# Two more weight slots, a scale moved behind the token gather, and a first gather split by groups of four experts, in a two-layer encoder kernel

## The chip, the cores and the metric

The kernel runs on one core of a Trainium2 chip. The metric is the device time of one execution in microseconds. The kernel before took 790.39 us, the median of three runs (790.09 to 791.79).

## The reference

The input is 256 tokens of 1024 features in f32, behind which 16 learned meta tokens are put in front, so T = 272. There are two layers: layer 0 mixes tokens with a gated convolution and a gated linear attention, layer 1 with grouped-query attention. Each ends with a mixture of experts (MoE), in which each token goes to the best of 4 groups and in it to the best 2 of 8 experts. Cut to what the change touches:

```python
def rms_norm(x, g):
    y = x * lax.rsqrt(jnp.mean(x * x, axis=-1, keepdims=True) + NORM_EPS)
    return y * g

def hierarchical_moe(h, w_group, b_group, w_expert, b_expert, w_gate, w_up, w_down):
    g_logits = xt @ w_group + b_group                 # 4 groups, softmax, the largest is taken
    e_logits = (xt @ w_expert + b_expert)             # 8 experts in each group, the best two are taken
    gates = ...                                       # softmax of the two, times the group's probability
    for e in range(32):                               # F = 256
        he = jax.nn.silu(xt @ w_gate[e]) * (xt @ w_up[e])
        out = out + gates[:, e:e + 1] * (he @ w_down[e])

for i in range(2):
    h = h + mixer_i(rms_norm(h, norm_mix[i]))
    h = h + hierarchical_moe(rms_norm(h, norm_ffn[i]), ...)   # layer 1: without the meta tokens
return rms_norm(h, norm_final)
```

## The kernel before

**The weights.** The 32 experts of a layer have 96 MB of f32 weights, in 96 units of 1 MB (`UNITS`): three for each expert (gate, up, down). They pass through a ring of 16 slots in SBUF (`RING`, `slots`). Slots 0 to 7 are also the ring of the mixers' weights, and slots 8 to 15 lie over the mixers' scratch memory. So the first 16 units of a layer can be loaded only as the mixer ahead of it lets go of those places (`first_units0`, `first_units1`).

**The stages.** Experts are worked off in 8 quads of four. A quad has three stages of four units each (gate, up, down), 24 stages in all; in the first quad the two first stages hold each the halves (over the input features) of gate and up. TensorE raises `stage_done` at the end of each stage. SyncE, which issues all weight DMAs in one queue, waits for it before it overwrites a slot: unit i waits for the stage of unit i - 16 (`rest_of_units`, the DMA lines 356 and 359, and 353 for the halves of the first quad). In the first stage that frees slots, unit 16 is thus issued.

**The tokens.** A quad takes at most 32 tokens for each expert (`SLOTS`). The router yields `key`, each token's rank in its expert's queue. `select` (line 1085) makes from it `sel`, a matrix of ones and zeros of 256 columns (8 experts, that is two quads, times 32 places). `gather` (line 1701) multiplies the normalized tokens `hn` with `sel`: hn is TensorE's stationary operand, taken as `hn[:, t, c:D:8]`, so 128 elements that lie 8 elements apart in each partition, and `sel` the moving one. For two quads it needs 8 feature chunks c times NT token tiles t of such products: NT is 3 in layer 0 (one tile is the 16 meta tokens) and 2 in layer 1. Each f32 matmul stands in the trace as two records, each with its own weight load. `x_out` copies the result from PSUM to `xT`, with ScalarE from bank 0 and VectorE from bank 1 (line 1122). The stages' matmuls stand at line 1652 (gate, up) and 1688 (down), the transposes of `he` at 1677, those of the weighted selection at 1711, the scatter back at 1726, and its addition to h at 1131.

**The order on TensorE in the first pair of quads**, of a layer: route (1606, 1607), logits (1621), ranks (1628), loads of the experts (1632), `gather` of feature chunks 0 to 3, first stage, `gather` of chunks 4 to 7, second stage, transposes, down stage of quad 0. Quad 1 finds its tokens gathered. Each later pair is gathered in one piece of 8 chunks during the odd quad before it.

**The router.** VectorE works off a chain of small instructions (lines 1033 to 1070), each of which waits for the one before it. ScalarE takes the roots for the norm (508) and the second half of the logits out of PSUM (672). The product `before` / `ones` times `chosen` counts for each token those ahead of it in its expert's queue.

**The norm.** `hn` = h * 1/rms * gain is made by VectorE at line 836 for all norms (`scale_tile`), the first tiles of the MoE's norm among the additions that end the mixer. The gain lies in a tile of 4 KB in each partition, which GpSimd's queue loads anew before each norm.

## Time and profile before

| | us |
|---|---|
| median of the runs | 790.39 |
| profiled execution, its own time | 789.43 |
| its span | 787.6 |
| TensorE, matmul busy | 651.5 (83%) |
| VectorE busy | 251.3 (32%) |
| ScalarE busy | 156.6 (20%) |
| DMA | 234.95 MB, mean 298 GB/s |

The profiled execution took 1.8 us more than its span, and 1.0 us less than the median. "Matmul busy" is no measure of a limit, since matmuls are pipelined and each record holds its latency. The second part of the page cuts the span into 40 slices of 19.7 us; the row GB/s shows when the weights stream. The MoE of layer 0 streams from about 199 to 399 us, that of layer 1 from about 569 to 768 us. Times in the trace are microseconds from the start of the span.

### The profile page before, as it was taken

How to read it: one execution, taken by the hardware profiler on the slowest of the kernel's cores; microseconds unless marked ns; L12 is line 12 of the kernel's file. 1: busy time of each engine (PE TensorE's matmuls, PEld its weight loads, DVE VectorE, ACT ScalarE, POOL GpSimd, SP SyncE). 2: the span in 40 equal slices, each digit the busy share in tenths (PEclk: the TensorE clock that was granted, in tenths of full speed). 3: DMA queues.
4: the chain of work that ended last, by engine and by line, in shares of the span. 5: the costliest groups of instructions: out<-in, count | busy, mean ns of one | idle time of the engine just before them, and what ended most of it. 6: DMA issues, size and time to landing. Idle time of an engine off the chain costs nothing.

```text
span 787.6 us, 10827 instructions
## 1 busy us (share of the span) xinstructions
PE 651.5 (83%) x4656; PEld 389.1 (49%) x4656; DVE 251.3 (32%) x582; ACT 156.6 (20%) x328; POOL 42.9 (5%) x40
## 2 busy tenths in 40 slices
PE   2999998987999599599589989798888587677665
PEld 2796997346574274274224345544635235235221
DVE  4255335144224033023033557603322212212204
ACT  4563350030100000000003235712101001001002
POOL 3222251000000000000000000000000000000000
PEclk9999999997999899699799998999799979879888
DMA  9641345980899999999994360079299999999991
GB/s 305 244 149 67 107 125 177 391 321 28 361 421 422 421 421 420 422 421 419 420 395 157 109 195 19 1 264 377 74 423 421 421 421 422 421 422 419 422 412 76
DMA packets 46041, 234.95 MB, mean 298 GB/s; under 512 B 4465, under 2 KB 4721, under 8 KB 23457
## 3 DMA queue, kind: packets, MB, share of 16 engines
q1 hardware_dynamic: 44720, 231.82, 73.9%
q0 software_dynamic: 1264, 2.34, 1.2%
q8 instruction: 41, 0.67, 0.3%
q14 instruction: 16, 0.12, 0.0%
HBM read 233.07 MB, written 1.05 MB: 297 GB/s over the span
## 4 chain that ended last, share of the span: by engine, by line
PE 64%; DMA 21%; DVE 5%; SPq 4%; ACT 3%; issue 2%; DVEq 0%; ACTq 0%
DMA ring<-in_moe_w_up 20%; PE bank L1701 10%; PE bank L1652 10%; PE bank L1726 6%; PE bank L1688 5%; SPq L356 4%; PE bank L1351 4%; PE bank L1560 4%; PE bank L1785 4%; PE bank L1893 4%; PE bank L1352 3%; PE bank L1353 3%; PE bank L1792 2%; ACT scratch L779 2%; DMA gain<-in_norm_mix 1%
## 5 line engine op out<-in xcount | busy, mean ns | idle before, releaser
L1652 PE MATMUL bank<-ring,hnT 128*32 128x256 f32 (+1 forms) x1920 | 141.0, 454 | 75.9 <-DMA ring<-in_moe_w_up 41.2
L1652 PEld LDWEIGHTS bank<-ring,hnT 128*32 128x32 f32 x1920 | 70.3, 126 | 148.7 <-issue 61.1
L1701 PE MATMUL bank<-sel,hn 128*128 128x256 f32 x320 | 83.4, 421 | 0.3 <-DVE sel L1085 0.3
L1701 PEld LDWEIGHTS bank<-sel,hn 128*128 128x128 f32 x320 | 79.5, 337 | 3.8 <-issue 1.7
L1726 PE MATMUL bank<-moe_scratch 128*128 128x512 f32 (+1 forms) x160 | 78.1, 611 | 1.8 <-ACT moe_scratch L696 1.6
L1142 DVE TENSOR_TENSOR moe_scratch<-moe_scratch,bank 128x256 f32<-128x256 f32 x16 | 6.7, 422 | 198.8 <-ACT moe_scratch L690 198.8
L1131 DVE TENSOR_TENSOR h<-bank,h 128x512 f32<-128x512 f32 (+1 forms) x80 | 55.1, 689 | 23.7 <-PE bank L1726 23.7
L1688 PE MATMUL bank<-ring,moe_scratch 128*32 128x512 f32 x512 | 58.2, 595 | 1.5 <-DMA ring<-in_moe_w_down 1.1
L1351 PE MATMUL bank<-hnT_hi,mix_hi 128*128 128x272 f32 x160 | 47.7, 298 | 1.7 <-DVE scratch L972 1.7
L1726 PEld LDWEIGHTS bank<-moe_scratch 128*128 128x128 f32 (+1 forms) x160 | 22.7, 169 | 50.2 <-issue 26.3
L1352 PE MATMUL bank<-hnT_hi,mix_lo 128*128 128x272 f32 x160 | 46.8, 293 | 0.0
L1353 PE MATMUL bank<-hnT_lo,mix_hi 128*128 128x272 f32 x160 | 46.7, 292 | 0.0
L690 ACT ACTIVATE moe_scratch<-bank 128x256 f32<-128x256 f32 x16 | 6.1, 384 | 199.1 <-PE bank L1652 199.1
L1122 DVE COPY hnT<-bank 128x512 f32<-128x512 f32 x16 | 11.1, 692 | 77.9 <-PE bank L1701 77.9
L1351 PEld LDWEIGHTS bank<-hnT_hi,mix_hi 128*128 128x128 f32 x160 | 30.8, 192 | 3.5 <-DVE scratch L972 2.0
L1688 PEld LDWEIGHTS bank<-ring,moe_scratch 128*32 128x32 f32 x512 | 15.4, 109 | 31.6 <-issue 30.8
L1353 PEld LDWEIGHTS bank<-hnT_lo,mix_hi 128*128 128x128 f32 x160 | 30.8, 193 | 0.0
L1352 PEld LDWEIGHTS bank<-hnT_hi,mix_lo 128*128 128x128 f32 x160 | 30.8, 192 | 0.0
L1560 PE MATMUL bank<-ring,hnT 128*128 128x512 f32 x64 | 28.3, 597 | 0.3 <-ACT hnT L660 0.3
L295 POOL TENSOR_TENSOR mix_lo<-ring,mix_hi 128x2048 fp32r<-128x2048 f32 x5 | 24.0, 4803 | 79.5 <-ACT mix_hi L564 79.5
L1893 PE MATMUL bank<-ring,hnT 128*128 128x512 f32 x64 | 27.7, 594 | 0.5 <-ACT hnT L792 0.5
L1785 PE MATMUL bank<-ring,hnT 128*128 128x512 f32 x64 | 28.0, 595 | 0.0
(272 smaller groups left out, 696.1 us busy)
## 6 DMA issues: line engine op xcount, KB each, us to landing
ring<-in_moe_w_down SPq DMA_DIRECT2D x64, 1024.0 KB, 26.7
ring<-in_moe_w_gate SPq DMA_DIRECT2D x56, 1024.0 KB, 21.7
ring<-in_moe_w_up SPq DMA_DIRECT2D x56, 1024.0 KB, 25.9
ring<-in_sc_w_in SPq DMA_DIRECT2D x12, 1024.0 KB, 12.4
ring<-in_moe_w_gate SPq DMA_DIRECT2D x16, 512.0 KB, 6.7
ring<-in_moe_w_up SPq DMA_DIRECT2D x16, 512.0 KB, 7.9
ring<-in_att_w_in SPq DMA_DIRECT2D x6, 1024.0 KB, 20.5
ring<-in_sc_w_out SPq DMA_DIRECT2D x4, 1024.0 KB, 6.8
```

Source lines behind the costliest of these rows:

```text
L356: sp.dma_start(dst.rearrange("p (c n) -> p c n", c=KC), src).then_inc(sem(f"weights{l}_{stage_of(i) % 4}"), 16)
L1131: nc.vector.tensor_tensor(hh, B[[7, 4][k % 2]][0:n, :], hh, ALU.add).then_inc(sem(f"h_added{l}"), 1)
L1351: mm(dst, left[0], right[0], start=start, stop=False)
L1352: mm(dst, left[1], right[0], start=False, stop=False)
L1353: return mm(dst, left[0], right[1], start=False, stop=stop)
L1560: last = mm(bank[:, :], hnT[:, c, TILE_AT[t]:TILE_AT[t] + P], out_weights(half, c), start=(c == 4), stop=(c == 3))
L1652: return mm(bank[at, :], xT[:, c, mine], right, start=(c == 0), stop=(c == KC - 1))
L1688: last = mm(B[5 + half][at, :], heT[:, c, at], w[j][:, c * D + half * W:c * D + half * W + W], start=(c == 0), stop=(c == 1))
L1701: last = mm(B[k % 2][:, 2 * P * cc:2 * P * cc + 2 * P], hn[:, t, c:D:KC], picks, start=(t == a), stop=(t == b - 1))
L1726: mm(B[[7, 4][k % 2]][0:m, :], selgT[:, TILE_AT[t]:TILE_AT[t] + m], y[:, half, :], start=True, stop=True).then_inc(sem(f"sc_ps{l}"), 1)
L1785: last = mm(bank[:, :], hnT[:, c, TILE_AT[t]:TILE_AT[t] + P], att_weights(2 * b + c // 4)[:, c % 4 * W:c % 4 * W + W], start=(c == 0), sto ...
L1893: last = mm(B[2 * half + i][:, :], hnT[:, c, i * P:(i + 1) * P], slots[u % MIX_RING][:, c % 4 * W:c % 4 * W + W], start=(c == 0), stop=(c ...
```

## The change

- **Slots.** `RING` becomes 18 units; the two new slots 16 and 17 lie in a tile `tail` of their own, over memory that in the mixer of layer 0 holds rounded weights. The memory comes from the gain tile, which goes away. The first units of a layer are loaded in another order and into other slots, since two more can be loaded. The semaphores of the stages go round in five instead of four.
- **Scaling.** `hn` of the MoE's norms is now h * 1/rms, made by ScalarE in one instruction for each tile, once VectorE has taken the reciprocals of all tiles in one instruction. The gain is multiplied in when the gathered tokens are taken out of PSUM (`x_first`, `x_out`): ScalarE by a scale for each partition, one chunk at a time, VectorE by a broadcast `tensor_tensor`. The gains of the first and the last norm lie in ring slots.
- **First gather.** The first pair's tokens are gathered for each quad by itself, with 128 columns of `sel`, in four parts (`first_gather`): quad 0, chunks 0 to 3; loads of the experts; first stage; quad 0, chunks 4 to 7; second stage; quad 1, both halves; then the transposes and the down stage of quad 0.
- **Selection.** The first `sel` is made in two halves of four experts; the second pair's is made during quad 0.
- **Ranks.** The rank product is three matmuls instead of six in layer 0, two instead of three in layer 1.
- **Router.** Four small instructions go: `padded` is a part of `logits` (the group's columns move behind the experts'), and the indices are compared as they are (lines 1052 and 1065 go); the subtraction at line 1046 comes later in the chain. Two roots and reciprocals for each tile become one for all.

```diff
-    RING = 16
+    RING, HOME = 18, 16
...
-    RING_ORDER = [list(range(RING)), [2, 3, 4, 5] + list(range(8, 16)) + [6, 7, 0, 1]]
+    RING_ORDER = [[16, 17, 8, 9, 10, 11, 0, 1, 2, 3, 4, 5, 6, 7, 12, 13, 14, 15],
+                  [16, 17, 2, 3, 4, 5, 8, 9, 10, 11, 12, 13, 14, 15, 6, 7, 0, 1]]
...
             def first_units0():
                 sp.wait_ge(sem("proj_ps"), PROJ["ac"] + 4)
-                unit(0, 0)
-                unit(0, 1)
+                for i in (6, 7):
+                    unit(0, i)
                 sp.wait_ge(sem("proj_ps"), PROJ["ab"] + 4)
-                unit(0, 2)
-                unit(0, 3)
+                for i in (8, 9, 0, 1):
+                    unit(0, i)
                 sp.wait_ge(sem("ybT_ps"), 3)
                 sp.wait_ge(sem("ya_ready"), 4)
-                for i in range(8, 16):
+                for i in (2, 3, 4, 5, 14, 15, 16, 17):
                     unit(0, i)
...
# layer 1, among the mixer's weights
+                    sp.wait_ge(sem("stage_done0"), more0 * NSTAGE + stage_of(last_user(0, HOME + 1)) + 1)
+                    unit(1, 0)
+                    unit(1, 1)
...
# ScalarE, moe(l)
+                act.wait_ge(sem("norm_var"), upto(n) + b - a)
+                nc.scalar.activation(stats[:, n, 2, a:b], stats[:, n, 1, a:b], ACT.Sqrt).then_inc(sem("norm_std"), b - a)
+                act.wait_ge(sem("norm_rcp"), l + 1)
+                for t in tiles:
+                    m = TILE_N[t]
+                    nc.scalar.activation(hn[0:m, t, :], h[0:m, t, :], ACT.Copy, scale=stats[0:m, n, 3, t:t + 1]).then_inc(sem("hn_ready"), 1)
...
# VectorE, moe(l)
-                link(nc.vector.tensor_copy(padded[:, a:b, 0:G], logits[:, a:b, 0:G]))
...
-                link(nc.vector.tensor_copy(gidx.unsqueeze(2), idx_g[:, a:b, 0:1]))
...
-                link(nc.vector.tensor_copy(rstat[:, 1:3, a:b], idx_e[:, a:b, 0:2].rearrange("p t k -> p k t")))
...
-                scale_tile(n, NT - 1, inverted=True)
...
-                select(0)
+                select(0, 4)
+                select(4, 4)
...
+                def x_first(r, n):
+                    dve.wait_ge(sem(f"x_ps{l}"), r * NXP + 2 * n + 2)
+                    k = n % 2
+                    nc.vector.tensor_tensor(xT[:, 4 * k + 2:4 * k + 4, n // 2 * P:n // 2 * P + P], FIRST_BANK[k][1][:, 0:2 * P].rearrange("p (c n) -> p c n", c=2),
+                                            gainT[:, l, 4 * k + 2:4 * k + 4].unsqueeze(2).to_broadcast([P, 2, P]), ALU.mult).then_inc(sem(f"x_dve{l}"), 1)
...
# TensorE, moe(l)
-                for t in tiles:
-                    for s in range(a, t + 1):
-                        m = TILE_N[s]
-                        last = mm(B[7][:, 32 * t:32 * t + 32], (before if s == t else ones)[0:m, :], chosen[0:m, s, :], start=(s == a), stop=(s == t))
-                last.then_inc(sem("rank_ps"), 1)
+                mm(B[7][:, 32 * a:96], before, chosen[:, a:b, :], start=True, stop=False, skip_group_check=True)
+                if a == 0:
+                    mm(B[7][:, 32:96], ones[0:NM, :], chosen[0:NM, 0, :].unsqueeze(1).to_broadcast([NM, 2, G * EPG]), start=False, stop=False, skip_group_check=True)
+                mm(B[7][:, 64:96], ones, chosen[:, 1, :], start=False, stop=True, skip_group_check=True).then_inc(sem("rank_ps"), 1)
...
+                def first_gather(r, q, half):
+                    pe.wait_ge(sem("hn_ready"), HN_BEFORE[n] + NT)
+                    pe.wait_ge(sem(f"sel{l}"), r * NSEL + q + 1)
+                    for k in range(2):
+                        for cc in range(2):
+                            c = 4 * half + 2 * k + cc
+                            for t in tiles:
+                                picks = sel[:, t, 4 * q:4 * q + 4, :].rearrange("p j s -> p (j s)")
+                                last = mm(FIRST_BANK[half][k][:, P * cc:P * cc + P], hn[:, t, c:D:KC], picks, start=(t == a), stop=(t == b - 1))
+                        last.then_inc(sem(f"x_ps{l}"), 1)
...
-                def all_but_last(r):
-                    gather(r, 0, (0, 1))
+                def all_but_last(r, first=False):
+                    first_gather(r, 0, 0)
+                    if first:
+                        expert_loads()
                     first_gate_up(r, 0)
-                    gather(r, 0, (2, 3))
+                    first_gather(r, 0, 1)
                     first_gate_up(r, 1)
+                    for half in range(2):
+                        first_gather(r, 1, half)
```

The waits of `down` in the first quad change too: it waits until VectorE has taken the last of the four parts out of PSUM, since bank 6 held it.

## Rows read from the trace of the kernel before

**Rows 1.** Page, second part: granted clock and rate in 40 slices.

```profile
PEclk9999999997999899699799998999799979879888
GB/s 305 244 149 67 107 125 177 391 321 28 361 421 422 421 421 420 422 421 419 420 395 157 109 195 19 1 264 377 74 423 421 421 421 422 421 422 419 422 412 76
```

**Rows 2.** Timeline of SyncE's queue, layer 0: start, us, line, what, count.

```profile
197.64 1.93 SPq L356 DMA_DIRECT2D ring<-in_moe_w_up  x4
208.16 1.99 SPq L359 DMA_DIRECT2D ring<-in_moe_w_down  x4
213.75 2.44 SPq L356 DMA_DIRECT2D ring<-in_moe_w_gate  x4
...
220.65 7.01 SPq L359 DMA_DIRECT2D ring<-in_moe_w_down  x4
242.14 1.75 SPq L356 DMA_DIRECT2D ring<-in_moe_w_gate  x4
```

**Rows 3.** Windows: stretch, length, busy of PE, PEld, DVE, ACT, POOL, clock, DMA, GB/s.

```profile
188.00:190.00 2.00, 2.00 (x7) 1.70 (x6) 0.18 (x1) 0.00 (x0) 0.00 (x0) 0.68 0.00 0
...
198.00:200.00 2.00, 2.00 (x10) 2.00 (x10) 0.00 (x0) 0.00 (x0) 0.00 (x0) 1.00 0.53 160
...
208.00:210.00 2.00, 1.00 (x9) 0.62 (x5) 0.44 (x2) 0.77 (x2) 0.00 (x0) 1.00 0.91 299
```

**Rows 4.** Timeline of the router, layer 0: start, us, engine, line, operation, tiles, shapes.

```profile
173.80 0.43 DVE L1033 COPY moe_scratch<-bank 36x272 f32<-36x272 f32 x1 [1.47 <-PE bank L1607]
...
174.55 0.39 ACT L672 ACTIVATE moe_scratch<-bank 36x272 f32<-36x272 f32 x1
...
176.64 0.17 DVE L1041 COPY moe_scratch<-moe_scratch 128x12 f32<-128x12 f32 x1
...
180.73 3.18 PE L1628 MATMUL bank<-moe_scratch,consts 16*128 16x32 f32 x12 [4.81 <-DVE moe_scratch L1070]
...
184.31 0.96 DVE L1085 TENSOR_TENSOR sel<-consts,moe_scratch 128x768 f32<-128x768 f32 x1
185.32 7.72 PE L1701 MATMUL bank<-sel,hn 128*128 128x256 f32 x24
...
193.94 3.64 PE L1652 MATMUL bank<-ring,hnT 128*32 128x512 f32 x32 [0.90 <-issue]
```

**Rows 5.** Timeline of the same stretch, from the second stage's end to the down stage.

```profile
208.59 0.42 DVE L1142 TENSOR_TENSOR moe_scratch<-moe_scratch,bank 128x256 f32<-128x256 f32 x1 [2.35 <-ACT moe_scratch L690]
209.07 0.51 PE L1677 MATMUL bank<-consts,moe_scratch 128*128 128x128 f32 x2 [0.95 <-DVE moe_scratch L1142]
...
210.04 3.64 PE L1688 MATMUL bank<-ring,moe_scratch 128*32 128x512 f32 x32
...
226.36 11.77 PE L1701 MATMUL bank<-sel,hn 128*128 128x256 f32 x48
```

**Rows 6.** Lines 1701 and 1893: durations in ns (least/median/largest), stretch, shapes.

```profile
L1701 PEld LDWEIGHTS bank<-sel,hn x48: 312/338/338, 226.2 to 237.5; 128*128 128x128 f32 x48
...
L1893 PEld LDWEIGHTS bank<-ring,hnT x64: 186/190/190, 516.0 to 542.7; 128*128 128x128 f32 x64
```

**Rows 7.** Page, fifth part: group of 64 records with contiguous weights, 512 columns.

```profile
L1785 PE MATMUL bank<-ring,hnT 128*128 128x512 f32 x64 | 28.0, 595 | 0.0
```

**Rows 8.** Timelines of layer 1: ranks, gather, and SyncE's queue.

```profile
553.65 1.49 PE L1628 MATMUL bank<-moe_scratch,consts 128*128 128x32 f32 x6 [4.05 <-DVE moe_scratch L1070]
...
556.26 6.28 PE L1701 MATMUL bank<-sel,hn 128*128 128x256 f32 x16 [0.27 <-DVE sel L1085]
...
567.13 2.17 SPq L356 DMA_DIRECT2D ring<-in_moe_w_up  x4
575.75 2.19 SPq L359 DMA_DIRECT2D ring<-in_moe_w_down  x4
```

**Rows 9.** Timelines: the last up stage of layer 0 and of layer 1.

```profile
392.36 6.17 PE L1652 MATMUL bank<-ring,hnT 128*32 128x256 f32 x64 [3.90 <-DMA ring<-in_moe_w_up]
...
761.22 3.66 PE L1652 MATMUL bank<-ring,hnT 128*32 128x256 f32 x64 [3.20 <-DMA ring<-in_moe_w_up]
```

More of the change, by code:

```diff
@@ L75, in down_stage, with last_user @@
         return gate_up_stages(q)[-1] + 1
+    def last_user(l, slot):
+        return max(i for i in range(NU) if RING_ORDER[l][i % RING] == slot)
     def landed(stage):
-        same = [16 * STAGES[k] * (2 if k < 2 else 1) for k in range(stage % 4, NSTAGE, 4)]
-        return sum(same[:stage // 4 + 1]), sum(same)
+        same = [16 * STAGES[k] * (2 if k < 2 else 1) for k in range(stage % NSEM, NSTAGE, NSEM)]
+        return sum(same[:stage // NSEM + 1]), sum(same)
     ctx = ExitStack()
@@ L96, in build_program @@
         hn = sb("hn", [P, 3, D])
-        gain = sb("gain", [P, D])
         with ExitStack() as plain:
-            ring = plain.enter_context(nc.sbuf_tensor("ring", [P, RING * UNIT], f32))
+            ring = plain.enter_context(nc.sbuf_tensor("ring", [P, HOME * UNIT], f32))
             hnT = plain.enter_context(nc.sbuf_tensor("hnT", [P, KC, T], f32))
-        slots = [ring[:, i * UNIT:(i + 1) * UNIT] for i in range(RING)]
+        slots = [ring[:, i * UNIT:(i + 1) * UNIT] for i in range(HOME)]
         mix_lo = [sb(f"mix_lo{i}", [P, UNIT], f32r) for i in range(MIX_RING)]
@@ L138, in build_program @@
         sel = sb("sel", [P, 3, 8, SLOTS])
+        tail = sb("tail", [P, (RING - HOME) * UNIT])
+        slots += [tail[:, i * UNIT:(i + 1) * UNIT] for i in range(RING - HOME)]
+        gain_first = slots[HOME + 1][:, UNIT - D:UNIT]
+        gain_last = slots[RING_ORDER[1][6]][:, 0:D]
         spent = [0]
@@ L221, in build_program @@
         logitsT = carve(1, T)[:, 0, :]
-        logits = carve(3, 36)
-        padded = carve(3, 8)
+        logits = carve(3, 40)
         top_g = carve(3, 8)
@@ L310, in states_done @@
             return k + 1 if k < 2 else 2 * k
+        FIRST_BANK = [(B[0], B[1]), (B[7], B[6])]
         LA_BANK = [0, 1, 2, 7]
@@ L377, in first_units0 @@
                     unit(0, i)
             def first_units1():
-                wait_mix_read(sp, 1, 1)
-                unit(1, 0)
-                unit(1, 1)
-                wait_mix_read(sp, 1, 2)
-                unit(1, 2)
-                unit(1, 3)
+                for i in (2, 3, 4, 5):
+                    if i % 2 == 0:
+                        wait_mix_read(sp, 1, i // 2)
+                    unit(1, i)
                 sp.wait_ge(sem("oT_ps"), 8)
-                for i in range(4, 12):
+                for i in range(6, 14):
@@ L390, in first_units1 @@
                     unit(1, i)
-                for i in range(12, 16):
+                for i in range(14, 18):
                     if i % 2 == 0:
-                        wait_mix_read(sp, 1, NMIX[1] - 2 + (i - 12) // 2)
+                        wait_mix_read(sp, 1, NMIX[1] - 2 + (i - 14) // 2)
                     unit(1, i)
@@ L525, in norm @@
                         squares(i, tiles[i])
-                        root(i)
                     for i in range(last):
@@ L533, in norm @@
                         squares(last, tiles[last])
-                    root(last)
                     return
@@ L690, in one_round @@
                         nc.scalar.activation(act_g, B[2][:, 0:F], ACT.Silu).then_inc(sem(f"silu{l}"), 1)
+                        if q == 0:
+                            x_first(r, 2)
+                            x_first(r, 3)
                         act.wait_ge(sem(f"heT_ps{l}"), base + q + 1)
@@ L824, in invert_root, with scale_tile @@
                 link(nc.vector.reciprocal(stats[0:m, n, 3, t:t + 1], stats[0:m, n, 2, t:t + 1]))
-            def scale_tile(n, i, inverted=False):
+            def scale_tile(n, i):
                 t = NORM_TILES[n][i]
                 m = TILE_N[t]
-                if not inverted:
-                    invert_root(n, i)
-                if i == 0 and n:
-                    dve.wait_ge(sem("gain_in"), {1: 16, 3: 32, 4: 48}[n])
-                elif i == 0:
-                    dve.wait_ge(sem("gain0_in"), 16)
+                invert_root(n, i)
+                if i == 0:
+                    dve.wait_ge(sem("gain_in"), {0: 16, 4: 32}[n])
+                gain = gain_last if n else gain_first
                 nc.vector.scalar_tensor_tensor(hn[0:m, t, :], h[0:m, t, :], stats[0:m, n, 3, t:t + 1], gain[0:m, :],
                                                ALU.mult, ALU.mult).then_inc(sem("hn_ready"), 1)
-            def norm_tile(n, i):
-                mean_square(n, i)
-                scale_tile(n, i)
             def norm(n):
@@ L1019, in _ @@
                 nc.vector.tensor_tensor(hh, got[0:n, :], hh, ALU.add).then_inc(sem("h_mixed0"), 1)
-                if half == 1 and t < 2:
-                    norm_tile(1, t)
             def moe(l):
@@ L1144, in one_round @@
                             add_tokens(base, q - 1)
+                        else:
+                            x_first(r, 2)
+                            x_first(r, 3)
                         if q % 2 and q + 1 < NQ:
-                            x_out(base, q // 2 + 1)
+                            x_out(r, q // 2 + 1)
                         dve.wait_ge(sem(f"selgT_ps{l}"), base + q + 1)
@@ L1306, in _ @@
                     nc.vector.tensor_tensor(hh, B[k][:, :], hh, ALU.add).then_inc(sem("h_mixed1"), 1)
-                    if half == 1 and i < 1:
-                        norm_tile(3, i)
             moe(1)
```

188 lines of the change are left out of this document (106 added, 82 removed).

## The prediction, made before the changed kernel ran

> **What bounds the kernel now.** I read the 40 slices first [rows 1]. While a layer's experts run, the rate stands at 420 to 422 GB/s in every full slice: the weights stream without a break, and TensorE waits for them. So a MoE ends when its last unit has landed, and the time is lost where the rate falls: slice 10 (28 GB/s) and slice 29 (74 GB/s), the two router gaps, in which the ring is full and no stage has yet been done. A unit of 1.049 MB takes 2.49 us at 421 GB/s. The second view was SyncE's queue, which shows when a stage's end frees four slots [rows 2, 8]: call the ends of the stages S0, S1, ... In layer 0 they are S0 = 197.64, S1 = 208.16, S2 = 213.75, S4 = 220.65, S5 = 242.14. The third were windows of 2 us [rows 3]. From 198 to 200 the rate is 160 GB/s, which is 0.76 us of full rate, so data flows from 199.24: 1.6 us behind the issue. From 208 to 210 it dips to 299: four units take 9.95 us, to 209.2, and those freed by S1 start at 208.16 + 1.6 = 209.76. After that no dip.
>
> This gives a rule: four units freed by Sk start at the later of Sk + 1.6 and the end of the four before. Before, the last constraint is S1, with 76 units behind it (80 in all less 4): 209.76 + 76 x 2.49 = 399.0 for layer 0. In layer 1 S0 binds alone (S1 = 575.75 comes in time): 567.13 + 1.6 + 80 x 2.49 = 767.9 [rows 8].
>
> **Two slots.** 18 units are in before the gap and 78 remain: 2 x 2.49 = 5.0 us less in each layer, if the stream behind is unbroken. Loading 18 instead of 16 fits the gap, 22 us long, and the waits for the old mixer weights stand in the same order; the two units more among the attention's weights go into slices at 109 to 195 GB/s [rows 1]. I cost both at nothing; without the cover each would cost up to 2.5 us a unit.
>
> **Router, layer 0** [rows 4]. (a) ScalarE's copy of the logits stood behind the last tile's root: it ends at 174.94. The root now comes later, so VectorE's own copy (1033, to 174.23) is last: 0.7 us. (b) The copy at 1041 costs 0.20 with its wait; two casts of the same size go too, and the subtraction (half hidden, 0.1) moves: 0.7. Comparing u32 with f32 is not in the trace; from 0 to 0.2 more for each of two places, I take 0. Chosen is there at 179.3, not 180.73. (c) Ranks: 12 records in 3.18, 0.265 each; 6 records give 1.6. (d) VectorE's scaling of the last tile lay beside the ranks: 0. Now ScalarE scales three tiles, 1.06 each as its squares of the same size, from 175 to 178.3, ahead of the gather by 3.6; nothing on the path. (e) Half a selection: 0.96 for 768 elements; 0.5 to 0.6 for 384. In sum the gather starts at 179.3 + 1.6 + 0.1 + 0.3 + 0.55 + 0.05 = 181.9 instead of 185.32, 3.4 us earlier.
>
> **The first gather: narrower, but not shorter.** This is where I chose. 128 columns of `sel` instead of 256 halve the moving side. Does that side set the time? 64 records of 512 columns take 28.0 us, 0.4375 each [rows 7]; 256 columns would be 0.22, 128 columns 0.11. But the gather's 48 records take 11.77 us at the full clock, 0.245 each, more than the 0.22 [rows 5], and its weight loads last 338 ns against 190 for contiguous weights of the same type and size [rows 6]. The load of `hn`, taken 8 elements apart, outlasts the columns. It stays as it is. So I take 0.243 for a record of 128 columns too; bounds are 0.135 (the rank's load of contiguous weights, 0.265 at half clock, halved) and 0.338 (a load that nothing hides). The Trainium skill, SBUF — State Buffer, Door 1, says that SBUF has lines of 16 bytes and each access that crosses to a new one pays a penalty; 8 f32 apart is 32 bytes. By that rule, the trace agrees with the longer load.
>
> Then the first gather costs as before, and quad 1 must be gathered anew: 48 records more in layer 0 and 32 in layer 1, 11.7 and 7.8 us, between the second stage and the down stage of quad 0. The clock: the ranks, after 4.81 us of waiting, and the gather's start ran at half clock (1.2 GHz); the granted clock of 0.68 in 188 to 190 puts the rise to 2.4 GHz at 189.3, 8.6 us after the ranks began [rows 3, 4]. TensorE's work now starts 1.4 us earlier but has a hole of 1 us between ranks and gather. With the rise between 187.8 and 190.4, the 24 records (0.475 at half clock, 0.243 at full) end between 190.6 and 191.9, at 191.2, not 193.04: 1.9 us earlier. The loads of the experts, 6 records, 0.8 us, hide VectorE's 0.42 for the evacuation [rows 5], where 0.90 passed before. The stage itself, 3.64. **S0 = 195.7.** Second quarter: as before, 10.52, less 0.27 for the smaller evacuation (0.42 for 0.69): **S1 = 206.0.**
>
> **S2 is the new constraint.** From S1: gathers of quad 1, 11.65; from the transposes of `he` to the down stage 0.97 (209.07 to 210.04), down to the issue 3.71 [rows 2, 5]. `he` is long there, so the wait of 0.9 ahead of the transposes goes. 11.65 + 0.97 + 3.71 = 16.3: **S2 = 222.3**, 8.5 later than before. The stream starts at 195.7 + 1.6 = 197.3, S1 is all but in time (207.6 for 207.25), and the third four could start at 217.5, but wait until 223.9: 6.4 us of standstill. Behind them 70 units: 223.9 + 174.3 = **398.2, against 399.0: 0.8 us won in layer 0**, out of 5.0 + 1.9. The next tight place is S5: S4 to S5 was 21.5; S2 to S4 6.9; so 250.7 + 1.6 = 252.3, due at 223.9 + 29.9 = 253.8. It holds by 1.5 us.
>
> **Layer 1** [rows 8], same steps with two tiles. Logits and chain 1.6, as in layer 0 within 0.2: ranks at 552.05 instead of 553.65. Four records for six: 1.0. Key 0.35, selection of 256 elements 0.4: gather at 553.9 instead of 556.26. 16 records, half clock until 560.6 (8.6 after the ranks, again without the hole) or up to 1.5 later: end near 561.0, not 562.55. S0 = 565.35 instead of 567.13, 1.8 earlier. S1 after 8.62 - 0.27: 573.7. S2 after 7.75 + 0.97 + 3.71: 586.1. The stream: 566.95, S1 in time; the third four could start at 586.85 and wait until 587.7. Then 70 units: 762.0 against 767.9: **5.9 us won.**
>
> **The rest, at nothing.** Both tails are set by the last up units, so they move with the stream; their clock is a lottery of 2.5 us: 64 records took 6.17 in layer 0, where the clock had fallen during a wait, and 3.66 in layer 1 [rows 9]. The gain of the last norm follows unit 95 in the queue, half a megabyte, 14 us before it is read. In the loop ScalarE takes two copies for one (0.2 more), beside a gather of 11.6 us. VectorE has queued behind `x_first`: the gates, 1.9 us, done during the first quarter; the load counts, during the first stage; the second selection, a quad before it is read. GpSimd and the DMA lose two gain loads, which fell into gaps.
>
> **Sum.** 0.8 + 5.9 = 6.7: span 780.9, profiled execution 782.7. The median shown stands 1.0 above the profiled execution: **783.6.**
>
> **The rivals.**
> (1) The columns bind (0.135 a record). Against it: 0.245 is above 0.22. The Trainium skill, TensorE: Matmul & The Clock Gate, LDWEIGHTS, says that a load takes P / 1.2 ns for P columns, whatever else; by that, 107 ns, it would hide, and the halved columns would show, but the 338 ns speak against it. From the rows alone: layer 0, gather from 181.9 to 188.4, S0 193.1, S1 200.7, S2 211.9: no standstill, end 194.7 + 194.2 = 388.9, 10.1 won. Layer 1: S0 563.6, end 759.4, 8.5 won. Time 771.8.
> (2) Slower: the strided load can be hidden only behind 256 columns, and with 128 a record costs up to 0.338. S2 then comes 96 x 0.095 = 9.1 later in layer 0 and 64 x 0.095 = 6.1 in layer 1, one for one on the stream: 798.8. It decides from 0.043 more a record on, 0.286. For it: the ranks' 32 columns still cost 0.265 a record, so a load is not free where few columns hide it. Against it: at 256 columns a record (0.245) is shorter than the load's own 338 ns, so loads overlap each other or what runs beside them.
> (3) TensorE falls further behind: the rise of the clock waits until the hole is 8.6 us past, or S5 passes its 1.5 us in layer 0. S0 later by 1 in both, S5 by 1 to 2 too: 786 to 789.
> (4) The slots bring nothing because the down stage of quad 0 waits in both layers for more than I see: 789 to 791.
>
> **How the numbers follow.** The forecast 0.66, 779.5 to 787.5 by the clock's rise (2 x 0.7), S2 (2 x 1) and the lottery of a tail (2.5). Rival (1) and values between 0.135 and 0.243: 0.14, from 771 to 779.5. (3): 0.08. (4): 0.04, within 0.2%. (2): 0.08, above 792. The range 776 to 789 leaves out most of rival (1) (0.10) and (2) with half of (4) (0.10). 0.2% is 1.6 us, about what a measurement of this kernel can tell from no change. Faster: 0.66 + 0.14 + 0.07 = 0.87; same 0.05; slower 0.08.
>
> **What would show it.** Right: in the first gather 0.24 us a record of 128 columns at full clock and loads of 338 ns; SyncE's third issue of a layer near 222 and some 13 us behind S1 in layer 1 (12.4); a hole in the rate of about 6 us before 224 in layer 0 and under 1 us in layer 1; S0 some 2 us earlier. Wrong: records of 0.13 (rival 1) or above 0.28 (rival 2), a hole near S5, or a first gather that begins later than 182.

## The result, and the profile after

The changed kernel took **778.79 us**, the median of 4 runs (775.6 to 780.62), against 790.24 (788.55 to 791.79) for the kernel before on the same chips: a ratio of 0.9851, interval 0.9813 to 0.9889. It is faster by 11.5 us, where 6.8 had been forecast. The profiled execution took 780.62 us, the longest of the four and 1.8 above their median; its span is 778.8.

The page of the changed kernel, second part (granted clock in tenths and rate, 40 slices of 19.5 us), which answers to [rows 1]:

```profile
PEclk9999999997999999799799999999899988879869
GB/s 301 254 145 73 109 126 131 378 413 69 407 297 421 420 422 420 422 421 421 418 396 279 113 196 16 1 247 375 122 406 422 421 419 422 421 421 421 420 372 56
```

Slices 10 and 29 are still the router gaps. Behind the first of them stands something new: 297 in slice 12, where the stream had started and stopped again.

SyncE's queue in the changed kernel (start, us, line, what, count), against [rows 2, 8]. An entry of four units whose slots came free two and two spans the wait between them:

```profile
192.74 0.80 SPq L369 DMA_DIRECT2D tail<-in_moe_w_up  x2
193.59 10.11 SPq L372 DMA_DIRECT2D ring<-in_moe_w_down  x4
203.74 15.96 SPq L369 DMA_DIRECT2D ring<-in_moe_w_gate  x4
...
247.29 0.80 SPq L369 DMA_DIRECT2D ring<-in_moe_w_gate  x2
...
539.76 0.80 SPq L369 DMA_DIRECT2D ring<-in_moe_w_up  x2
558.60 0.80 SPq L369 DMA_DIRECT2D tail<-in_moe_w_up  x2
```

S0 is at 192.74 in layer 0 (197.64 before) and at 558.60 in layer 1 (567.13 before). TensorE's timeline of layer 0 and of layer 1, against [rows 4, 5, 8]. Line 1663 and those behind it are the ranks, 1743 the first gather, 1672 the loads of the experts, 1692 gate and up, 1731 the down stage; the entry of line 688 is ScalarE's scaling of `hn`:

```profile
174.46 3.22 ACT L688 ACTIVATE hn<-h,stats 16x1024 f32<-16x1024 f32 x3 [0.24 <-DVE stats L1065]
178.89 0.74 PE L1663 MATMUL bank<-moe_scratch,consts 128*128 128x96 f32 x2 [4.12 <-DVE moe_scratch L1094]
...
181.92 6.10 PE L1743 MATMUL bank<-sel,hn 128*128 128x128 f32 x24 [1.11 <-DVE sel L1108]
187.95 1.16 PE L1672 MATMUL bank<-moe_scratch,consts 16*128 16x32 f32 x6
...
192.61 6.02 PE L1743 MATMUL bank<-sel,hn 128*128 128x128 f32 x24
199.20 3.64 PE L1692 MATMUL bank<-ring,hnT 128*32 128x512 f32 x32 [0.56 <-issue]
202.77 11.73 PE L1743 MATMUL bank<-sel,hn 128*128 128x128 f32 x48
215.20 3.64 PE L1731 MATMUL bank<-ring,moe_scratch 128*32 128x512 f32 x32
...
550.20 4.08 PE L1743 MATMUL bank<-sel,hn 128*128 128x128 f32 x16 [0.95 <-DVE sel L1108]
```

Windows of the changed kernel (length, busy of PE, PEld, DVE, ACT, POOL, granted clock, DMA share, GB/s), against [rows 3]:

```profile
184.00:186.00 2.00, 2.00 (x10) 2.00 (x10) 0.09 (x1) 0.62 (x2) 0.00 (x0) 0.50 0.00 0
...
188.00:190.00 2.00, 2.00 (x19) 1.32 (x22) 1.16 (x5) 0.00 (x0) 0.00 (x0) 0.90 0.00 0
214.00:216.00 2.00, 1.91 (x16) 1.12 (x19) 1.29 (x3) 0.38 (x1) 0.00 (x0) 1.00 0.39 164
216.00:218.00 2.00, 2.00 (x24) 0.65 (x20) 0.45 (x1) 0.00 (x0) 0.00 (x0) 1.00 0.02 8
218.00:220.00 2.00, 2.00 (x36) 0.96 (x32) 0.69 (x1) 0.60 (x1) 0.00 (x0) 1.00 0.25 29
220.00:222.00 2.00, 2.00 (x44) 1.23 (x40) 0.00 (x0) 0.00 (x0) 0.00 (x0) 1.00 0.68 254
...
580.00:582.00 2.00, 2.00 (x44) 1.17 (x36) 0.00 (x0) 0.00 (x0) 0.00 (x0) 1.00 0.81 299
```

The loads of its first gather and of quad 1's (ns, least/median/largest, and the stretch), against [rows 6]:

```profile
L1743 PEld LDWEIGHTS bank<-sel,hn x24: 312/338/338, 181.9 to 187.4; 128*128 128x128 f32 x24
L1743 PEld LDWEIGHTS bank<-sel,hn x48: 313/335/338, 202.8 to 214.0; 128*128 128x128 f32 x48
```

Two things are to be seen. First, the three gathers of layer 0 take 6.10 us for 24 records, 6.02 for 24 and 11.73 for 48: 0.254, 0.251 and 0.244 a record. These means hold the longer start of each group; behind its first record, the starts of the records stand 0.240 apart in the first gather and 0.238 to 0.240 in the others. Yet the first ran wholly at half clock (0.50 until it ended at 188.0), the others at full clock. A record of 128 columns costs the same at either clock, and so does its load, 335 to 338 ns. Second, the stream stops: S2 = 215.20 + 3.64 = 218.84, and the four windows from 214 to 222 carry 455 of 4 x 421 GB/s: (1684 - 455) x 2 / 421 = 5.8 us are missing. In layer 1 the window 580 to 582 carries 299, and 582 to 584 carries 406: 0.65 us are missing there.

**Where the time went**, by the profiles. Layer 0's last up stage begins at 388.62 instead of 392.36 [rows 9], so the stream won 3.7. In layer 1 the same stage begins 11.9 earlier (749.34 for 761.22), and its mixer had ended 4.0 earlier (539.76 in the queue above; the entry of the same units before was at 543.79), so the stream of layer 1 won 7.9. The tails moved with the clock: the last up stage took 3.65 in layer 0 and 6.4 in layer 1, where [rows 9] have 6.17 and 3.66. Layer 0's tail thus won 2.5, layer 1's lost 2.7. Between them the attention lost 2.3. Of this, 0.9 went at full clock in its first projection (line 1851), which waited 0.66 for VectorE's `hnT`; it waits so in e1 and e4 too, but not in e9 or the kernel before, so the two slots, which e4 lacks, are not its cause. The cause and the rest of the 2.3 are open. 3.7 + 2.5 - 2.3 + 7.9 - 2.7 = 9.1, against 787.6 - 778.8 = 8.8 of span.

The first entries of the last up stages in the timeline of the changed kernel, and the attention's projection:

```profile
388.62 0.41 PE L1692 MATMUL bank<-ring,hnT 128*32 128x256 f32 x2 [1.46 <-DMA tail<-in_moe_w_up]
...
418.47 3.70 PE L1851 MATMUL bank<-ring,hnT 128*128 128x512 f32 x8 [0.66 <-DVE hnT L1219]
...
749.34 0.64 PE L1692 MATMUL bank<-ring,hnT 128*32 128x256 f32 x2 [3.65 <-DMA tail<-in_moe_w_up]
```

A window within the up stage of layer 1, at half clock:

```profile
750.00:752.00 2.00, 2.00 (x24) 0.88 (x20) 0.00 (x0) 0.00 (x0) 0.00 (x0) 0.50 1.02 426
```

### The profile page after: what moved, and what is told of

It is laid out like the page before. It is cut to its first block, busy times and chain, and to the rows that moved or that the text cites. A ratio compares the mean times of both kernels' runs of the same rounds, so it can differ in the third digit from the quotient of the medians.

```text
span 778.8 us, 11001 instructions
## 1 busy us (share of the span) xinstructions
PE 661.6 (85%) x4728; PEld 402.7 (52%) x4728; DVE 243.5 (31%) x571; ACT 166.5 (21%) x354; POOL 41.3 (5%) x37
## 4 chain that ended last, share of the span: by engine, by line
PE 67%; DMA 18%; DVE 6%; SPq 4%; ACT 3%; issue 2%; DVEq 0%; ACTq 0%
PE bank L1692 11%; DMA ring<-in_moe_w_up 10%; PE bank L1756 7%; DMA tail<-in_moe_w_up 7%; PE bank L1781 7%; PE bank L1743 5%; PE bank L1731 5%; PE bank L1389 4%; PE bank L1598 4%; SPq L369 4%; PE bank L1844 4%; PE bank L1952 4%; PE bank L1390 3%; PE bank L1391 3%; ACT scratch L814 2%
## 5 line engine op out<-in xcount | busy, mean ns | idle before, releaser
L1692 PE MATMUL bank<-ring,hnT 128*32 128x256 f32 (+1 forms) x1568 | 138.4, 453 | 57.3 <-DMA ring<-in_moe_w_gate 24.6
L1692 PEld LDWEIGHTS bank<-ring,hnT 128*32 128x32 f32 x1568 | 67.4, 126 | 116.3 <-issue 45.2
L1756 PE MATMUL bank<-sel,hn 128*128 128x256 f32 x240 | 59.1, 406 | 0.0
L1756 PEld LDWEIGHTS bank<-sel,hn 128*128 128x128 f32 x240 | 58.0, 337 | 0.0
L1692 PE MATMUL bank<-tail,hnT 128*32 128x256 f32 (+1 forms) x352 | 48.5, 433 | 1.8 <-DMA ring<-in_moe_w_gate 1.5
L1743 PE MATMUL bank<-sel,hn 128*128 128x128 f32 x160 | 39.9, 416 | 2.1 <-DVE sel L1108 2.1
L1743 PEld LDWEIGHTS bank<-sel,hn 128*128 128x128 f32 x160 | 38.7, 336 | 5.6 <-issue 5.6
L1598 PE MATMUL bank<-ring,hnT 128*128 128x512 f32 x64 | 28.3, 597 | 0.3 <-ACT hnT L670 0.3
L1692 PEld LDWEIGHTS bank<-tail,hnT 128*32 128x32 f32 x352 | 21.6, 119 | 12.9 <-issue 5.6
```

The lines of the kernel that those rows point to most:

```text
L1598: last = mm(bank[:, :], hnT[:, c, TILE_AT[t]:TILE_AT[t] + P], out_weights(half, c), start=(c == 4), stop=(c == 3))
L1692: return mm(bank[at, :], xT[:, c, mine], right, start=(c == 0), stop=(c == KC - 1))
L1743: last = mm(FIRST_BANK[half][k][:, P * cc:P * cc + P], hn[:, t, c:D:KC], picks, start=(t == a), stop=(t == b - 1))
L1756: last = mm(B[k % 2][:, 2 * P * cc:2 * P * cc + 2 * P], hn[:, t, c:D:KC], picks, start=(t == a), stop=(t == b - 1))
```

## The experiments

**Theory A.** A record has two limits, and the larger counts. The load of `hn` at a stride of 8 elements costs it 0.24 us at either clock. Its columns take twice as long at half clock: 256 of them 0.43, above the load, 128 of them no more than it. So the narrow first gather wins where the clock is low (8.58 us in e1 against 6.10 in layer 0, 5.39 against 4.08 in layer 1), and at full clock it wins nothing; its second half, quad 1, then stands ahead of the down stage and holds the stream back at S2. The two slots bring their 10 us all the same, since they move every limit. The rivals B to G stand in the expectations.

### e1: the first gather once, 256 columns wide

The parts of the first gather, written as a list of (first quad, number of quads, half of the chunks):

```diff
-[(0, 1, 0), (0, 1, 1), (1, 1, 0), (1, 1, 1)]
+[(0, 2, 0), (0, 2, 1)]
```

> The changed kernel (778.79 us), but its first gather is made once for both quads with 256 columns, in two halves of the chunks as in the kernel before; all else stays. Theory A (the records of the gather are bound by the strided weight load, 0.243 us at the full clock whatever the columns; the extra gathers hold up the down stage of quad 0, whose end S2 restarts the stream): first half ends near 191.2 instead of 187.95, because at half clock 256 columns take 0.475 a record; S0 3 us later in layer 0 and 1.8 later in layer 1, S2 7 us earlier in layer 0; no standstill of the stream there. 70 units behind S2 become 74 behind S1: 2.8 us won in layer 0, 1.3 lost in layer 1: 777.3 us. Rival B (the narrow first gather is what brings the gain, by its earlier S0): 783 to 784 us.

**775.86 us** (773.62 to 776.95), ratio 0.9816 [0.9794, 0.9838]: faster than the change by 3 us. TensorE in this kernel:

```profile
182.53 8.58 PE L1747 MATMUL bank<-sel,hn 128*128 128x256 f32 x24 [1.58 <-DVE sel L1110]
...
208.10 3.64 PE L1733 MATMUL bank<-ring,moe_scratch 128*32 128x512 f32 x32
```

Of the 24 wide records, those before the clock's rise near 188.5 start 0.427 apart, those behind it 0.24. The gather is 2.5 longer and starts 0.6 later, behind a selection of twice the size, so S0 comes 3.0 later than in the changed kernel (195.69). But S2 comes at 211.7 instead of 218.84, ahead of its due time. S1, near 206.1, binds: the third four start at 206.1 + 1.6 + 9.96 = 217.7 instead of 220.5. The split costs more than it wins, as A has it; rival B, under which it is worth having, is out. The interval of this ratio overlaps a little with that of the change; the same step at 16 slots (e9 against e4), where they lie apart, costs 2.9.

### e2: narrow only where the clock is low

```diff
-[(0, 1, 0), (0, 1, 1), (1, 1, 0), (1, 1, 1)]
+[(0, 1, 0), (0, 2, 1), (1, 1, 0)]
```

> The changed kernel, but only quad 0's chunks 0 to 3 are gathered with 128 columns; chunks 4 to 7 are gathered once for both quads with 256 columns, and quad 1's chunks 0 to 3 come behind the second stage, 24 records less in layer 0 and 16 less in layer 1. Theory A: S0 unchanged (192.7), a record of 256 columns at full clock costs as much as one of 128 (0.243), S2 5.2 us earlier in layer 0, the standstill there falls from 5.5 to under 1 us: 5.2 us won in layer 0, 0.6 in layer 1: 773.0 us. Rival B (what counts is S0, and the later standstill is given back elsewhere): 778 to 779 us.

**774.89 us** (773.5 to 775.74), ratio 0.9802 [0.9782, 0.9822]. TensorE in this kernel:

```profile
181.57 6.09 PE L1747 MATMUL bank<-sel,hn 128*128 128x128 f32 x24 [1.11 <-DVE sel L1110]
...
192.13 6.13 PE L1747 MATMUL bank<-sel,hn 128*128 128x256 f32 x24
...
202.66 5.97 PE L1747 MATMUL bank<-sel,hn 128*128 128x128 f32 x24
```

Here is the comparison in one kernel: at full clock 24 records of 256 columns take 6.13, of 128 columns 5.97; at half clock 24 of 128 columns take 6.09. S0 is early (192.26) and S2 too (213.0). It is 3.9 us below the change (3.5 below e5, the change run once more), 1.9 above what A expected; against e1 the intervals overlap, so that it beats e1 isn't shown.

### e3: hn stored chunk by chunk, so that the load is contiguous

```diff
-nc.scalar.activation(hn[0:m, t, :], h[0:m, t, :], ACT.Copy, ...)
+nc.scalar.activation(hn[0:m, t, :].rearrange("q (c p) -> q c p", c=KC),
+                     h[0:m, t, :].rearrange("q (p c) -> q c p", c=KC), ACT.Copy, ...)
...
-hn[:, t, c:D:KC]
+hn[:, t, P * c:P * c + P]
```

> The changed kernel with hn stored in another order: ScalarE reads h 8 elements apart and writes each chunk's 128 features side by side, and the gather's weight loads read 128 contiguous elements. Theory A (the stride bounds the record): loads of 190 ns instead of 338, records of 128 columns 0.13 to 0.14 us at full clock, 0.265 at half clock, records of 256 columns 0.22. S1 2.6 us earlier and S2 7 us earlier in layer 0, no standstill: 6 us won in layer 0, 0.3 in layer 1: 772.5 us. Rival C (an f32 record costs 0.243 for a reason other than the stride, such as the selection's or the accumulation's form): 0.243 stays, 778.8 us, or later if ScalarE's strided read takes over 2 us a tile and delays the gather.

**769.61 us** (766.85 to 771.24), ratio 0.9733 [0.9709, 0.9758]. The loads of the gathers in this kernel:

```profile
L1743 PEld LDWEIGHTS bank<-sel,hn x24: 192/333/334, 180.0 to 184.4; 128*128 128x128 f32 x24
L1743 PEld LDWEIGHTS bank<-sel,hn x48: 186/192/193, 196.3 to 201.5; 128*128 128x128 f32 x48
```

Its timeline, ScalarE's scaling and the gathers:

```profile
172.54 6.22 ACT L688 ACTIVATE hn<-h,stats 16x1024 f32<-16x1024 f32 x3 [0.24 <-DVE stats L1065]
180.00 4.80 PE L1743 MATMUL bank<-sel,hn 128*128 128x128 f32 x24 [1.11 <-DVE sel L1108]
189.20 2.94 PE L1743 MATMUL bank<-sel,hn 128*128 128x128 f32 x24
196.28 5.63 PE L1743 MATMUL bank<-sel,hn 128*128 128x128 f32 x48
```

Its windows:

```profile
182.00:184.00 2.00, 2.00 (x12) 2.00 (x11) 0.24 (x1) 0.62 (x2) 0.00 (x0) 0.51 0.00 0
184.00:186.00 2.00, 2.00 (x17) 1.59 (x20) 0.65 (x3) 0.00 (x0) 0.00 (x0) 1.00 0.00 0
```

At full clock a record falls from 0.244 to 0.117 (5.63 / 48), and its load from 338 to 192 ns. The starts stand 0.112 apart instead of 0.240. At half clock little changes: of the first 24 records, 19 begin before the rise at 184, 0.213 apart instead of 0.240, with loads of 333 ns. So the stride is what binds at full clock. At half clock 128 columns alone take 0.213, just under the 0.240 of the strided load, so halving the columns there brings a record all the way down to the load's limit. Rival C is out. With the second gather at 5.6 instead of 11.7, S2 is at 206.3 and nothing stops. It won 2.9 us more than A expected. In this profile the mixer of layer 0 ended 1.9 earlier than in the changed kernel's; whether it does so in the median is not shown.

By the Trainium skill, SBUF — State Buffer, Door 1, each crossing to a new 16-byte line of SBUF costs; 8 f32 are 32 bytes. The trace agrees: 338 ns against 192 at full clock.

### e4: the change without the two slots

```diff
-RING, HOME = 18, 16
+RING, HOME = 16, 16
```

with the loading order of before; the last two units' memory holds only the gain.

> The changed kernel with 16 slots and the loading order of the kernel before; all else stays. Theory A: S0, S1, S2 unchanged within a layer, two units more behind each: 5.0 us more in each layer, 788.8 us. Rival D (the slots bring little, since the standstill before S2 eats what was loaded ahead): 779 to 784 us.

**789.41 us** (786.32 to 791.55), ratio 0.9986 [0.9972, 1.0]. A window of this kernel:

```profile
216.00:218.00 2.00, 2.00 (x24) 0.65 (x20) 0.50 (x1) 0.00 (x0) 0.00 (x0) 1.00 0.00 0
```

The slots are worth 10.3 to 11.0 us, whichever of the two measurements of the changed kernel (above and e5) is taken, by ratio or by median; the count gives 2 x 4.98. Rival D is out. Everything else in the change together is worth 1.1 us and hardly to be told from nothing. The standstill stands at the same place with and without the slots: the third four wait for S2 in both, and with two slots more 70 units instead of 72 are left behind it.

### e5: the changed kernel once more

> The changed kernel once more, unchanged, so that it stands on the same chip and beside the same runs of the kernel before as the others of this set: 778.8 us, ratio 0.985. It tells by how much the variants with another first gather differ from it.

**778.42 us** (775.86 to 781.77), ratio 0.9856 [0.9833, 0.988]: the base for e6 to e8, beside which it ran. In its profile, the slowest of its six runs (781.77), the clock rose at 185.7, within the first gather, and the 24 records still took 5.97. It fell once more in the second stage, which took 5.33 instead of 3.64, and S2 came at 220.69: what the stage loses there, the stream loses.

### e6: a third gather's worth ahead of the down stage

```diff
-for cc in range(2):
+for cc in range(2 * (2 if (q, half) == (1, 0) else 1)):
+    cc = cc % 2
```

Quad 1's gather of chunks 0 to 3 is computed twice.

> The changed kernel with one cost doubled: quad 1's gather of chunks 0 to 3, behind the second stage, is computed twice (the second time over the first), 24 records more in layer 0 and 16 in layer 1. Theory A (the end of the down stage of quad 0 restarts the stream, one for one): 24 x 0.243 = 5.8 us in layer 0 and 16 x 0.243 = 3.9 us in layer 1 more: 788.5 us. Rival B (TensorE's work there is covered by the ring's 18 units): 779 to 781 us.

**787.6 us** (784.17 to 790.8), ratio 0.9975 [0.9956, 0.9993]. TensorE in this kernel:

```profile
202.99 17.43 PE L1744 MATMUL bank<-sel,hn 128*128 128x128 f32 x72
...
221.12 3.64 PE L1731 MATMUL bank<-ring,moe_scratch 128*32 128x512 f32 x32
```

24 records more in layer 0 and 16 in layer 1, at 0.244, are 9.8 us on TensorE; the kernel lost 9.2. S2 comes at 224.76, 5.9 later, and from 222 to 224 nothing flows. Layer 0 alone could give only 5.9 of the 9.2. TensorE's work between S1 and S2 thus counts almost one for one: S2 binds, in both layers.

### e7: the clock held up by unused products

```diff
 last.then_inc(sem("logits_ps"), 1)
+for _ in range(4 if l == 0 else 3):
+    mm(B[2][:, :], ones, consts[:, 0:W], start=True, stop=True)
```

and one more behind the ranks; their results are not used.

> The changed kernel with TensorE kept busy while VectorE routes: four (layer 1: three) matmuls of ones with 512 columns behind the logits, one behind the ranks, into a bank that nobody reads. Theory A': the clock stays at 2.4 GHz through the gap; the strided load takes 0.243 us at either clock, so the first gather gains only 0.2 us, ranks and expert loads 1.2 us: S0 1.4 us earlier in each layer, 776.0 us. Rival E (all of TensorE's work scales with the clock, as the prediction had it): the first gather would take 2.9 us instead of 6.0, S0 4 us earlier, 771 to 773 us.

**774.92 us** (773.6 to 776.26), ratio 0.982 [0.9797, 0.9842]. TensorE in this kernel:

```profile
180.74 5.99 PE L1746 MATMUL bank<-sel,hn 128*128 128x128 f32 x24 [0.17 <-DVE sel L1108]
```

Its windows:

```profile
178.00:180.00 2.00, 1.53 (x8) 1.11 (x8) 0.79 (x5) 0.87 (x3) 0.00 (x0) 1.00 0.13 53
180.00:182.00 2.00, 1.83 (x7) 1.29 (x6) 1.79 (x8) 0.00 (x0) 0.00 (x0) 0.76 0.05 8
182.00:184.00 2.00, 2.00 (x11) 2.00 (x9) 0.84 (x4) 0.00 (x0) 0.00 (x0) 0.50 0.00 0
184.00:186.00 2.00, 2.00 (x10) 2.00 (x10) 0.00 (x0) 0.63 (x2) 0.00 (x0) 0.89 0.00 0
```

The clock was full for the ranks, fell during the gather all the same, and came back: full, half and full in one gather, and its 24 records still took 5.99. Rival E, under which they would take 2.9, is out: the time of the strided gather doesn't depend on the clock; layer 1's, wholly at full clock here, took 4.04 for its 16 records, against 4.08 mostly at half clock in the changed kernel. The 3.5 us that were won are not all accounted for. S0 came 1.5 earlier, 0.4 of it because the mixer of layer 0 ended earlier in this profile and 1.1 by the faster ranks, loads and gather; in layer 1 the same steps won 0.5. The other 1.9 stay open.

### e8: contiguous, with the clock held up

The edits of e3 and e7 together.

> Contiguous loads of hn and a busy TensorE together. Theory A': with 128 contiguous elements a record takes 0.25 us at half clock and 0.117 at full clock, so here the clock counts: the first gather 2.8 us instead of 4.8, ranks and loads 1.2 us less, S0 some 3 us earlier in each layer than with contiguous loads alone (769.6 us): 763.5 us. It must then wait for hn, which ScalarE writes in 2.07 us a tile when it reads with a stride: if that comes late, 1 us of it is lost in layer 0. Rival: 768 to 770 us, if the end of the gap is set by something other than TensorE.

**765.65 us** (764.57 to 766.22), ratio 0.9701 [0.9678, 0.9724]: the fastest version, 24 us below the kernel before. TensorE in this kernel:

```profile
180.52 2.92 PE L1746 MATMUL bank<-sel,hn 128*128 128x128 f32 x24 [0.17 <-DVE sel L1108]
```

Its windows:

```profile
180.00:182.00 2.00, 1.83 (x14) 1.51 (x14) 1.18 (x4) 1.64 (x4) 0.00 (x0) 1.00 0.04 8
182.00:184.00 2.00, 2.00 (x18) 1.84 (x17) 1.78 (x8) 0.63 (x2) 0.00 (x0) 1.00 0.00 0
```

Contiguous and at full clock the same 24 records take 2.92 instead of 6.10, S0 is at 187.96, and in layer 1 at 545.41. The sum by the stream's rule: the third four start at 187.96 + 1.6 + 19.9 = 209.5 instead of 220.5 (11.0), layer 1's S0 is 2.2 further ahead and its standstill of 0.6 is gone: 13.8, of which 0.6 is an earlier end of layer 0's mixer in this profile, and 12.8 were measured. The expectation (763.5) was 2.2 too low.

### e9: 16 slots and the wide gather

The edits of e4 and e1 together.

> The 16 slots and the loading order of the kernel before, with everything else of the change, but the first gather once with 256 columns for both quads. With 16 slots and the split gather the kernel took 789.4 us, 1.1 under the kernel before. Theory A: that is so little because the split gather gives back what the earlier router wins: the third end of a stage (S2) near 219 held the stream back. With the wide gather S0 comes near 195.7, S1 near 206.1 and binds: the stream behind it starts at 207.7 instead of 209.76, 2.1 us won in layer 0; in layer 1 S0 comes 2.8 us earlier and binds. Together 4.9 us: 785.5, 784 to 787. Rival F: the earlier router wins next to nothing with 16 slots, whichever way the first gather is made, because what it wins goes back at the layers' ends: 788.5 to 790.5.

**785.49 us** (783.28 to 787.57), ratio 0.9949 [0.9934, 0.9965]. SyncE's queue in this kernel:

```profile
194.11 1.97 SPq L369 DMA_DIRECT2D ring<-in_moe_w_up  x4
204.64 1.97 SPq L372 DMA_DIRECT2D ring<-in_moe_w_down  x4
210.22 2.42 SPq L369 DMA_DIRECT2D ring<-in_moe_w_gate  x4
```

S0 and S1 are each 3.5 earlier than in [rows 2], of which 1.5 is an earlier end of layer 0's mixer in this profile, and S2 is in time. Rival F is out: the rest of the change is worth 4.1 us without the split, and 1.1 with it. The pieces add up: two slots 10.5 here (the ratio of this one less that of e1) and 10.3 in e4 (against e5); the split costs 2.9 with 16 slots and 3.2 with 18.

### e10: contiguous, clock held up, and the wide gather

The edits of e1 and e8 together.

> The version with hn stored in contiguous chunks and unused products that hold the clock (765.65 us), but with the first gather once with 256 columns for both quads. Theory A: with contiguous loads a record costs what its columns cost, some 0.12 us for 128 columns and 0.22 for 256. The wide gather's first part then takes 24 x 0.22 = 5.3 us instead of 2.9, and S0 comes 2.4 us later in layer 0 and 1.6 later in layer 1; nothing stands still in either version, so all of it counts: 769.6, 768 to 771. Rival G: S0 is not what the stream waits for any more, or the wide gather wins back 3.4 us later from a down stage without a second gather ahead of it: 764 to 767.

**770.97 us** (768.9 to 773.32), ratio 0.9767 [0.9744, 0.9791]. TensorE in this kernel:

```profile
182.31 5.42 PE L1750 MATMUL bank<-sel,hn 128*128 128x256 f32 x24 [0.64 <-DVE sel L1110]
```

The sign of the split turns. A contiguous record of 256 columns takes 0.226 in the mean, nearly twice the 0.122 of 128 columns, so quad 1's share can be put off behind S0, 24 x 0.104 = 2.5 us in layer 0 and 1.7 in layer 1, and being short it no longer holds S2 back. The split now wins 5.3 us: these 4.2, and a gather that begins behind half a selection, 0.5 a layer. In the profiles S0 of layer 0 is 4.4 later than in e8; 1.3 of this is the mixer's later end, the other 3.0 are the selection and the gather. With strided loads it lost 3. Rival G is out.

## Why the prediction was right, and where it was off

The sign and the range of the forecast held, and so did the slots, the stream's rule and S2 as the new constraint; its gain of 6.8 us was too small by 4.7.

**Where the 4.7 come from.** In the profile the streams won 3.7 + 7.9 instead of 0.8 + 5.9, 4.9 more than forecast, by the step named below and an earlier rise of the clock in layer 1. The attention's 2.3, which the forecast had at nothing, and the two tails took 2.5 of that back, so that the span is only 2.1 below the forecast one (778.8 for 780.9). The rest of the error is no step of the kernel: the forecast set the median 1.0 above the profiled execution, as it had stood before, and here it stands 1.8 below it. How near the number came is thus partly chance.

**What bounds it.** Right. The rate stands at 420 to 422 in the full slices after the change too, and the rule with the measured ends gives the layers' ends: layer 0 220.4 + 70 x 2.49 = 394.7 against 399.0, 4.3 earlier by the rule and 3.7 in the trace. In layer 1 it gives 754.9 against 767.9, 9.0 earlier when the mixer's 4.0 are taken off, and the trace shows 7.9; this 1.1 is not explained.

**Slots, 5.0 a layer, the loads hidden.** Right: 10.3 to 11.0 for both (e4), 10.5 (e9).

**The router.** The gather was to start at 181.9 and started at 181.92, partly by two errors that cancel. Chosen came at 178.89, not 179.3, since the mixer ended 0.4 earlier in this profile; the ranks took 1.92 (178.89 to 180.81), not 1.6: their records with more columns cost more than the 0.265 of those with 32. ScalarE's scaling ended at 177.7, 4.2 ahead of the gather, hidden as stated.

**The record of the narrow gather: right at full clock, wrong at half.** This is the step that failed. At full clock the forecast was 0.243, and 0.244 to 0.251 was measured; S2 - S1 was to be 16.3 and was 16.0. At half clock I kept the 0.475 of the wide gather, as though the load alone set it there too, and the record cost 0.254. The 24 records ended at 188.0 instead of 191.2. Nearly the whole error of layer 0 is this term: S0 3.0 earlier than forecast (192.74 for 195.7), S1 3.1 (202.85 for 206.0), S2 3.5 (218.84 for 222.3), stream 3.7 won for 0.8. How much the columns did is shown by e1, with wide records in the same place: 2.5 us. The other 0.7 is not the columns: the clock rose near 188.4, somewhat earlier than assumed, and even wide records start 0.427 apart behind the first, not 0.475. In layer 1 the 16 records took 4.08 instead of 7.1, but in e1 the wide ones took 5.39 there. So 1.3 is the columns; most of the other 1.7 is the clock, which rose at 553.6, 5.4 behind the start of the ranks, where the forecast had 8.6 from layer 0. The stream of layer 1 won 7.9 for 5.9. The trace of before held the sign of it. Durations of the kernel before in its stretch at half clock (ns, least/median/largest):

```profile
L1701 PEld LDWEIGHTS bank<-sel,hn x10: 312/339/339, 185.3 to 188.9; 128*128 128x128 f32 x10
L1701 PE MATMUL bank<-sel,hn x9: 558/634/820, 185.3 to 188.9; 128*128 128x256 f32 x9
```

The loads there are not longer than those at full clock in [rows 6], while the starts of the records stand 0.427 apart, against 0.24 behind the rise. So the load did not set it at half clock; that left the columns, and columns are what the change halves. e3 and e7 showed the two limits apart: with the stride gone little changes at half clock (0.213 for 0.240), and with the clock up nothing changes while the stride stays.

**Rival (1), the columns bind**, was thus half right: at half clock. It was dismissed from records at full clock alone. At full clock it is wrong with strided loads and right with contiguous ones (e3: 0.117 for 0.243).

By the Trainium skill, TensorE: Matmul & The Clock Gate, LDWEIGHTS, a load takes about P / 1.2 ns for P columns, with no term for stride or clock, which for 128 columns gives an estimate of 107 ns. The trace disagrees: 338 ns strided, 192 contiguous at full clock, 333 at half.

**Rival (2), an unhidden load** (0.338 a record): out; the records with loads of 0.338 stand 0.24 apart.

**S2 as the new constraint.** Right, with its place and its size: a standstill of 5.8 us, forecast 6.4; under a microsecond in layer 1. e6 confirms it by adding to it. S5 was not late: 247.29, 28.4 behind S2 as forecast, and no window there dips.

**Rivals (3) and (4).** Neither happened: the clock rose near 188.4 in layer 0, in the earlier half of the range assumed, and at 553.6 in layer 1, and the slots paid.

**The tails.** The lottery of 2.5 us fell twice, once each way, and cancelled. That they cancelled is luck. Both signs are in one profile, so the 9.1 there is a less certain number than the 11.5 of the medians.

**What the forecast didn't ask.** It saw that the split turns S2 into the constraint, and took that as the price of an earlier S0. It could have set the two beside each other. With its own numbers, in which a narrow record costs as much as a wide one, the split wins only half a selection at S0 (0.45) and the smaller evacuation at S1 (0.27), and it moves the third four's start from about 218 to 223.9. e1 and e9 show the same change without the split faster by 3 us.

## What to carry to other kernels

When an operation has two limits, one in clock cycles and one in time, price it once for each clock that it runs at: a row at full clock says nothing of which limit holds at half. Before halving a matmul's columns, look whether its weight load outlasts them; if a stride makes it do so, lay the operand out contiguously first, for only then did it pay here to put off half of the columns (e10). And in a kernel bound by a stream through a ring of slots, slots pay by count, while a stage that starts earlier pays only until the next stage's end is late.

## What the runs showed of the hardware

- An f32 load of 128 columns, 8 elements apart, takes 338 ns at either clock; a contiguous one takes 192 at full clock and 333 at half.
- The starts of the gathers' f32 records stand this far apart (us, behind the first of a group; the runs in brackets). The means by record in the text are a little longer, since they hold the group's start and end:

| load of 128 f32 | columns | full clock | half clock |
|---|---|---|---|
| 8 elements apart | 128 | 0.238 to 0.240 (the changed kernel) | 0.240 (the changed kernel) |
| 8 elements apart | 256 | 0.240 (e2) | 0.427 (e1) |
| contiguous | 128 | 0.112 (e3, e8) | 0.213 (e3) |
| contiguous | 256 | 0.216 (e10) | in no trace |

- ScalarE pays for the stride too. Reading `h` 8 elements apart and writing it side by side, three tiles took 6.22 us instead of 3.22 (e3; the two accesses were not changed one at a time). In e3 `hn` was ready 1.2 before the gather, in e8 0.5 (173.81 + 6.23 for 180.52): nearly all of the cover is used.
- Unused matmuls between the router's steps kept the granted clock at 1.00 until the gather began, but with the strided gather behind them it fell to 0.50 within it (e7), and with the contiguous one it stayed at 1.00 (e8). In layer 1 of e7 it stayed at 1.00 with the strided gather too, so the stride alone does not decide it. Why these differ is not shown.
